# Two passes of 256 columns, in two banks, for the last 128 tokens of a decoder trunk's last product

## The chip, the cores and the metric

The kernel runs on one core of a Trainium2 chip. Its engines work side by side and wait for each other through semaphores: TensorE (PE in the profile) multiplies, with its weight loads shown apart as PEld; VectorE (DVE), ScalarE (ACT) and GpSimd (POOL) do elementwise work; SyncE (SP) issues transfers. The metric is the device time of one execution in microseconds (us); a kernel's time is the median of its runs.

## The reference

The input is 256 tokens of 2048 float32 features. Two layers follow each other, each with a token mixer (block attention in the first, retention in the second) and a gated feed-forward part. What ends the computation, and what the change touches, is this:

```python
def layer_norm(x, g, b):
    mu = xf.mean(-1, keepdims=True)
    var = jnp.square(xf - mu).mean(-1, keepdims=True)
    return ((xf - mu) * lax.rsqrt(var + LN_EPS)).astype(x.dtype) * g + b
...
    f = conv_ffn(h, ...)            # ... gelu(g) * val, w_out: (256 x 5632) @ (5632 x 2048)
    h = layer_norm(DEEPNORM_ALPHA * h + f, ln_g[i, 1], ln_b[i, 1])
```

## The kernel before

The 256 tokens are two tiles of 128 (TT = 2, tile index t); token t*128+p lives in partition p of `h[:, t]`. A matrix product is made in blocks of 512 output columns (COLS), and a block's rows of weights come in chunks of 256 rows by 512 columns. SP loads a chunk into one of four slots of `raw`; ACT rounds it to `w_hi` (L663), DVE subtracts to get the rest, `w_lo` (L943), and PE multiplies. Every product of the matrices is three matmuls: high by high, high by low and low by high (L328, L330, L331 in `multiply_tile`), each with 128 tokens of the activations as the stationary operand and 512 columns of weights as the moving one, accumulated in a bank of PSUM of 128 x 512 float32. `acc_a`, `acc_b`, `acc_c` and `mid` are pairs of such banks, one per token tile; `acc_a` and `acc_b` are the two halves of the tensor `acc_ab`, `acc_c` and `mid` those of `acc_cm`.

The last product of the program (`last_product`) is the fourth block of 512 columns of the second feed-forward part, 22 chunks into `acc_b`. The first 14 chunks are multiplied for both tiles as they arrive. The last eight are held on the chip: four in a place of their own (`early_hi`, `early_lo`, split ahead by L961) and four in the ring. PE passes over the eight chunks first for tile 0, then for tile 1. A pass is 8 chunks x 2 x 3 = 48 matmuls. Behind the first pass it signals `first_tile`, behind the second `products`.

DVE closes each tile in `last_layer_norm`: `last_residual` waits for the tile's signal, computes h = ALPHA*h + acc_b (L1079), takes the statistics of the last 512 columns (L1085), and joins the four blocks' statistics into mean and variance (L1088). GpSimd makes the reciprocal root from it (L917, L920). DVE meanwhile subtracts the mean and multiplies by the gain (`center`, L1094), and then scales and adds the bias (`scale_shift`, L1102), block by block; SP and ACT store each finished block (L285) in turn. `STORES` cuts tile 1's last block into two pieces of 256 columns. DVE and the other engines run their instructions strictly in the order written.

Of the kernel before, what the change touches and what calls it, by code (L numbers as in the profile page):

```python
# [24 lines left out]
ALU = mybir.AluOpType  # L25
# [3 lines left out]
P = 128  # L29
D = 2048  # L30
SEQ = 256
DEPTH = 2
TT = SEQ // P
KT = D // P
COLS = 512
CK = 2
CHUNK = CK * COLS
RING = 4
# [7 lines left out]
FSTEPS = F // COLS  # L46
NBLK = D // COLS
ALPHA = float((2 * DEPTH) ** 0.25)
# [17 lines left out]
TOKENS, FEATURES = (0, 0), (32, 48)  # L66
SLOT = CHUNK + 64
AHEAD = 4
FIRST_DONE = [None, 1, 2, 3, 4]
# [3 lines left out]
HCH = FT // CK  # L73
XQ, RQ = XCH // RING, RCH // RING
OQ = 2 * HCH // RING
# [11 lines left out]
Q_OUT1 = Q_FFN1 + 2 * FSTEPS * XQ - 1  # L87
TURNS = Q_OUT1 + NBLK // 2 * OQ


EARLY_FROM = [None, (Q_WO + 2 * XQ, XCH), (Q_OUT0 + OQ, HCH + 12), (Q_RWO + 3 * RQ, RCH - 2 * RING),
              (Q_OUT1 + OQ, HCH + 6)]
# [17 lines left out]
NC_FFN1 = NC_RET + RHEADS  # L110
# [4 lines left out]
B_USED = [None, NB_OUT0, NB_RET, NB_OUT1, NB_OUT1 + NBLK // 2]  # L115
# [4 lines left out]
def position(i, early):  # L120

    return i if early is None or i < early else i + min((i - early) // 2, RING)
# [8 lines left out]
def build_trunk(nc, x, weights, attn_tab, causal, ident_in, ret_tab, decay_tab, conv_in, ln_g, ln_b, out):  # L131
    with ExitStack() as ctx:
        def sb(name, shape, dt=F32):
            return ctx.enter_context(nc.sbuf_tensor(name, shape, dt))

        def sem(name):
            return ctx.enter_context(nc.semaphore(name))


        h = sb("h", [P, TT, D])  # L140
# [5 lines left out]
        w_lo = sb("w_lo", [P, RING, SLOT], F32R)  # L146
        conv_par = sb("conv_par", [P, DEPTH, 2 * FT, 4])
        ident = sb("ident", [P, P])
        ln_stats = sb("ln_stats", [P, TT, NBLK, 6])
        ln_mv = sb("ln_mv", [P, TT, 2])  # L150
        ln_ve = sb("ln_ve", [P, TT])
        ln_rstd = sb("ln_rstd", [P, TT])
# [42 lines left out]
        hid_hi, hid_lo = views(arena_at, ("hid_hi", [P, FT, SEQ], F32R), ("hid_lo", [P, FT, SEQ], F32R))  # L195
# [20 lines left out]
        acc_a, acc_b, acc_c, mid = acc_ab[:, 0:2], acc_ab[:, 2:4], acc_cm[:, 0:2], acc_cm[:, 2:4]  # L216

        def parts(s, place):

            return [w[:, s, at:at + CHUNK].rearrange("p (k n) -> p k n", k=CK)  # L220
                    for w, at in zip((w_hi, w_lo), place)]
# [27 lines left out]
        ln_params_in = sem("ln_params_in")  # L249
        out_stored = sem("out_stored")  # L250
        hi_ready = sem("hi_ready")
        lo_ready = sem("lo_ready")
        products = sem("products")
        first_tile = sem("first_tile")
        a_free, b_free, c_free = sem("a_free"), sem("b_free"), sem("c_free")
# [19 lines left out]
        tile0_turned, tile0_hi, tile0_ready = sem("tile0_turned"), sem("tile0_hi"), sem("tile0_ready")  # L275
        rv_rounded, s_rounded, s_ready = sem("rv_rounded"), sem("s_rounded"), sem("s_ready")
        half_set, idle_set = sem("half_set"), sem("idle_set")

        block = ctx.enter_context(nc.Block())

# [38 lines left out]

        @block.tensor  # L320
        def _(pe):
            def multiply_tile(acc, t, weight_parts, xh, xl, kt, first):

                o = acc[:, t]
                c = slice(t * P, (t + 1) * P)
                wh, wl = weight_parts
                for k in range(CK):
                    pe.matmul(o, xh[:, kt + k, c], wh[:, k], start=first and k == 0, stop=False,  # L328
                              skip_group_check=True)
                    pe.matmul(o, xh[:, kt + k, c], wl[:, k], start=False, stop=False, skip_group_check=True)  # L330
                    done = pe.matmul(o, xl[:, kt + k, c], wh[:, k], start=False, stop=True,  # L331
                                     skip_group_check=True)
                return done
# [25 lines left out]
            def product(turn, chunks, acc, free, used, xh, xl, feature_major, slots={}, ready=None, at=0,  # L359
                        early_at=None, held=None, first=0):  # L360


                if free is not None:
                    pe.wait_ge(free, used)
                hold = 0 if held is None else RING

                def count(s):
                    return RING * turn + position(at + s, early_at) + 1

                def counts(s):  # L370
                    return position(at + s + 1, early_at) - position(at + s, early_at)

                for s in range(chunks - hold):
                    if ready is not None:
                        pe.wait_ge(ready[0], ready[1](s))
                    multiply(acc, count(s), (at + s) % RING, xh, xl, CK * (first + s), feature_major,
                             first + s == 0, counts(s))
                    for step in slots.get(s, ()):
                        step()
                if hold:  # L380
                    for s in range(chunks - hold, chunks):
                        pe.wait_ge(lo_ready, count(s))
                        done = multiply_tile(acc, 0, parts((at + s) % RING, TOKENS), xh, xl, CK * s, False)
                    done.then_inc(first_tile, 1)
                    for s in range(chunks - hold, chunks):
                        multiply_tile(acc, 1, parts((at + s) % RING, TOKENS), xh, xl, CK * s,
                                      False).then_inc(products, counts(s))
                        for step in held.get(chunks - s, ()):
                            step()

            def last_product(turn, used):

                eh, el = early[4]
                split = HCH - 2 * RING

                def count(s):
                    return RING * turn + position(HCH + s, EARLY_FROM[4][1]) + 1

                product(turn, split, acc_b, b_free, used, hid_hi, hid_lo, False, at=HCH, early_at=EARLY_FROM[4][1])
                pe.wait_ge(lo_ready, early_position(4, RING - 1) + 1)  # L400
                for t in range(TT):
                    for s in range(RING):
                        done = multiply_tile(acc_b, t, (eh[:, s], el[:, s]), hid_hi, hid_lo, CK * (split + s), False)
                    for s in range(RING):
                        pe.wait_ge(lo_ready, count(split + s))
                        done = multiply_tile(acc_b, t, parts((HCH + split + s) % RING, TOKENS), hid_hi, hid_lo,
                                             CK * (split + RING + s), False)
                    done.then_inc((first_tile, products)[t], (1, RING)[t])

            def x_tiles(stage):  # L410
                return (x_ready, lambda s: PIECES * stage + s + 2)
# [527 lines left out]
        def _(dve):  # L939
# [45 lines left out]
            wh, wl = parts(0, FEATURES)  # L985
# [88 lines left out]
            def last_residual(stage, t, done, count, wait=True):  # L1074


                c = slice(D - COLS, D)
                dve.wait_ge(done, count)
                dve.scalar_tensor_tensor(out=h[:, t, c], in0=h[:, t, c], scalar=ALPHA, in1=acc_b[:, t],  # L1079
                                         op0=ALU.mult, op1=ALU.add).then_inc(b_free if t else summed, 1)  # L1080
                if t == 0:
                    dve.wait_ge(summed, NBLK * stage)
                else:
                    dve.wait_ge(b_free, B_USED[stage])
                dve.bn_stats(ln_stats[:, t, NBLK - 1], h[:, t, c]).then_inc(ln_stat, 1)  # L1085

                dve.wait_ge(ln_stat, TT * NBLK * stage - 1 + t)
                dve.bn_aggr(ln_mv[:, t], ln_stats[:, t].rearrange("p a s -> p (a s)")).then_inc(ln_mean, 1)  # L1088
                if wait:
                    dve.wait_ge(ln_mean, TT * (stage - 1) + t + 1)  # L1090

# [5 lines left out]
            def scale_shift(stage, part, t, c):  # L1097

                dve.wait_ge(ln_part, PART_BEFORE[stage] + part + 1)
                if c.start == 0:  # L1100
                    dve.wait_ge(ln_scale, TT * (stage - 1) + t + 1)
                dve.scalar_tensor_tensor(out=h[:, t, c], in0=h[:, t, c], scalar=ln_rstd[:, t:t + 1],  # L1102
                                         in1=ln_bias[:, c], op0=ALU.mult, op1=ALU.add).then_inc(ln_done, 1)
# [44 lines left out]

            def last_layer_norm(stage):

                dve.wait_ge(ln_params_in, 32 * NBLK * stage)
                for t, (done, count) in ((0, (first_tile, FIRST_DONE[stage])), (1, (products, RING * TURNS))):
                    mine = [i for i in range(len(STORES)) if STORES[i][0] == t]
                    last_residual(stage, t, done, count)
                    center(stage, mine[0], *STORES[mine[0]])
                    for i in mine:
                        if i + 1 in mine:
                            center(stage, i + 1, *STORES[i + 1])
                        scale_shift(stage, i, *STORES[i])

            def x_slots():

# [266 lines left out]
```

## Time and profile before

| What | Value |
|---|---|
| median of 3 runs | 2611.12 us (2610.8 to 2611.41) |
| the profiled execution's own time | 2612.95 us |
| its span, first to last instruction | 2611.2 us |
| mean granted TensorE clock | 0.999 |
| PE busy | 2598.4 us, 100% of the span |
| DVE, ACT, POOL busy | 1606.7, 1200.9, 15.9 us |

The span is shorter than the execution's own time by 1.75 us, which lie around it. Most of the program is one uninterrupted row of matmuls; what can be won or lost in the part looked at here are the PE passes up to the last matmul, and the work of DVE, GpSimd and the stores behind it.

### The profile page before, as it was taken

The numbers are of one execution on the slowest core, as the hardware profiler recorded it, in microseconds if no ns is written. First come the engines' busy times: TensorE is split into PE (matmuls) and PEld (weight loads), VectorE is DVE, ScalarE is ACT, GpSimd is POOL, SyncE is SP. The second block draws the span as 40 slices with busy tenths as digits, with TensorE's granted clock in tenths as the row PEclk, the third lists the DMA queues.
The fourth block names the chain that finished last, engine by engine and source line by source line (L and its number), as shares of the span: only waits on it lengthen the run. The fifth ranks groups of instructions, "written<-read, shape, count | busy, mean of one in ns | idle before, by whom it ended". The sixth has DMA issues, their size and how long they took to land.

```text
span 2611.2 us, 40543 instructions
## 1 busy us (share of the span) xinstructions
PE 2598.4 (100%) x14360; PEld 2265.8 (87%) x14360; DVE 1606.7 (62%) x1810; ACT 1200.9 (46%) x1348; POOL 15.9 (1%) x39
## 2 busy tenths in 40 slices
PE   9999999999999999999999999999999999999998
PEld 9999888888888888888888888888888888888886
DVE  6566667666676654565555555555766666665455
ACT  4444444555555543444444344433455555554332
POOL 0000000000000000000000000000000000000000
PEclk9999999999999999999999999999999999999999
DMA  6555574555555566655555555566555555556554
GB/s 226 180 166 166 172 252 146 194 186 191 193 186 191 189 230 193 206 186 181 179 174 181 181 177 179 181 216 198 170 193 181 194 183 193 192 193 229 195 188 153
DMA packets 140860, 493.92 MB, mean 189 GB/s; under 512 B 15472, under 2 KB 18032, under 8 KB 140784
## 3 DMA queue, kind: packets, MB, share of 16 engines
q1 hardware_dynamic: 133552, 481.49, 56.0%
q10 hardware_dynamic: 7232, 11.37, 1.4%
q8 instruction: 54, 0.88, 0.1%
q14 instruction: 22, 0.18, 0.0%
HBM read 490.70 MB, written 2.10 MB: 189 GB/s over the span
## 4 chain that ended last, share of the span: by engine, by line
PE 99%; DVE 0%; POOL 0%; ACT 0%; issue 0%; DVEq 0%; POOLq 0%
PE acc_cm L421 12%; PE acc_ab L331 12%; PE acc_ab L328 12%; PE acc_ab L330 12%; PE acc_ab L421 11%; PE acc_cm L424 6%; PE acc_ab L424 6%; PE acc_ab L342 5%; PE acc_ab L345 5%; PE acc_ab L344 5%; PE acc_cm L331 3%; PE acc_cm L328 3%; PE acc_cm L330 3%; PE acc_cm L484 0%; PE acc_cm L614 0%; PE acc_cm L635 0%
## 5 line engine op out<-in xcount | busy, mean ns | idle before, releaser
L943 DVE TENSOR_TENSOR w_lo<-raw,w_hi 128x1024 fp32r<-128x1024 f32 x895 | 1086.2, 1223 | 803.5 <-ACT w_hi L663 796.3
L663 ACT ACTIVATE w_hi<-raw 128x1024 fp32r<-128x1024 f32 (+1 forms) x897 | 934.9, 1055 | 877.6 <-PE acc_ab L331 447.1
L421 PE MATMUL acc_cm<-x_parts,w_hi 128*128 128x512 f32 x1408 | 489.4, 392 | 0.0
L421 PE MATMUL acc_ab<-x_parts,w_hi 128*128 128x512 f32 x1280 | 444.6, 392 | 0.0
L424 PE MATMUL acc_cm<-x_parts,w_lo 128*128 128x256 f32 x1408 | 394.3, 280 | 0.0
L424 PE MATMUL acc_ab<-x_parts,w_lo 128*128 128x256 f32 x1280 | 358.4, 280 | 0.0
L421 PEld LDWEIGHTS acc_cm<-x_parts,w_hi 128*128 128x128 f32 x1408 | 264.4, 188 | 57.8
L342 PE MATMUL acc_ab<-x_parts,w_hi 128*128 128x256 f32 x1024 | 291.1, 284 | 0.8 <-DVE w_lo L943 0.8
L345 PE MATMUL acc_ab<-x_parts,w_lo 128*128 128x256 f32 x1024 | 286.8, 280 | 0.0
L421 PEld LDWEIGHTS acc_ab<-x_parts,w_hi 128*128 128x128 f32 x1280 | 240.3, 188 | 52.6
L344 PE MATMUL acc_ab<-x_parts,w_hi 128*128 128x256 f32 x1024 | 285.8, 279 | 0.0
L328 PE MATMUL acc_ab<-w_hi,hid_hi 128*128 128x512 f32 x688 | 267.8, 389 | 0.0
L330 PE MATMUL acc_ab<-w_lo,hid_hi 128*128 128x512 f32 x688 | 267.7, 389 | 0.0
L331 PE MATMUL acc_ab<-w_hi,hid_lo 128*128 128x512 f32 x688 | 267.6, 389 | 0.0
L424 PEld LDWEIGHTS acc_cm<-x_parts,w_lo 128*128 128x128 f32 x1408 | 265.4, 189 | 0.1
L424 PEld LDWEIGHTS acc_ab<-x_parts,w_lo 128*128 128x128 f32 x1280 | 241.3, 188 | 0.0
L342 PEld LDWEIGHTS acc_ab<-x_parts,w_hi 128*128 128x128 f32 x1024 | 192.5, 188 | 1.5 <-issue 1.0
L344 PEld LDWEIGHTS acc_ab<-x_parts,w_hi 128*128 128x128 f32 x1024 | 192.7, 188 | 0.5
L345 PEld LDWEIGHTS acc_ab<-x_parts,w_lo 128*128 128x128 f32 x1024 | 192.5, 188 | 0.0
L330 PEld LDWEIGHTS acc_ab<-w_lo,hid_hi 128*128 128x128 f32 x688 | 129.1, 188 | 26.8
L331 PEld LDWEIGHTS acc_ab<-w_hi,hid_lo 128*128 128x128 f32 x688 | 129.1, 188 | 26.8
L328 PEld LDWEIGHTS acc_ab<-w_hi,hid_hi 128*128 128x128 f32 x688 | 129.1, 188 | 26.8
(142 smaller groups left out, 2976.6 us busy)
## 6 DMA issues: line engine op xcount, KB each, us to landing
raw<-in_weights_dram SPq DMA_DIRECT2D x911, 512.0 KB, 4.1
ln_gain<-in_ln_g_dram ACTq DMA_DIRECT2D x16, 256.0 KB, 4.6
ln_bias<-in_ln_b_dram ACTq DMA_DIRECT2D x16, 256.0 KB, 6.1
h<-in_x_dram SPq DMA_DIRECT2D x3, 512.0 KB, 8.9
decay_sb<-in_decay_tab_dram ACTq DMA_DIRECT2D x1, 1024.0 KB, 6.9
out_dram<-h SPq DMA_DIRECT2D x4, 256.0 KB, 2.5
out_dram<-h ACTq DMA_DIRECT2D x3, 256.0 KB, 2.5
raw<-in_weights_dram SPq DMA_DIRECT2D x2, 256.0 KB, 3.8
```

What stands on the lines that cost most here:

```text
L328: pe.matmul(o, xh[:, kt + k, c], wh[:, k], start=first and k == 0, stop=False, skip_group_check=True)
L330: pe.matmul(o, xh[:, kt + k, c], wl[:, k], start=False, stop=False, skip_group_check=True)
L331: done = pe.matmul(o, xl[:, kt + k, c], wh[:, k], start=False, stop=True, skip_group_check=True)
L342: pe.matmul(o, wh[:, k, c], xh[:, kt, :], start=first and f % 2 == 0, stop=False, skip_group_check=True)
L344: pe.matmul(o, wh[:, k, c], xl[:, kt, :], start=False, stop=False, skip_group_check=True)
L345: last = pe.matmul(o, wl[:, k, c], xh[:, kt, :], start=False, stop=True, skip_group_check=True)
L421: pe.matmul(acc[:, f], wh[:, k, c], x_parts[:, CK * s + k].rearrange("p a n -> p (a n)"), start=s == 0 and k == 0, stop=False, skip_group_ ...
L424: last = pe.matmul(acc[:, f, SEQ:2 * SEQ], wl[:, k, c], x_hi[:, CK * s + k, :], start=False, stop=True, skip_group_check=True)
L663: return act.activation(o, i, ACT.Copy)
L943: dve.tensor_tensor(wl, raw[:, at % RING], wh.bitcast(F32), ALU.subtract).then_inc(lo_ready, 1)
```

## The change

Tile 0's pass stays as it is. Tile 1's pass over the eight held chunks becomes two passes, each over the same eight chunks and over all their rows: the first multiplies the left 256 of the 512 columns into the first bank of `acc_c`, the second the right 256 into the second bank of `acc_c`, both starting from zero. The sum of tile 1 is thus in two places: the 14 chunks before in `acc_b[:, 1]`, the held eight in `acc_c`. DVE adds the first part, with ALPHA*h, as soon as the 14 chunks are done, in an instruction that now stands ahead of tile 0's closing work. It adds each half of 256 columns when its pass ends, takes each half's statistics by itself, and joins five sets of statistics in place of four for tile 1. `ln_stats` grows by one set a tile, which moves the tensors behind it by 64 bytes in each partition.

```diff
-        ln_stats = sb("ln_stats", [P, TT, NBLK, 6])
+        ln_stats = sb("ln_stats", [P, TT, NBLK + 1, 6])
...
+        first_half, half_summed = sem("first_half"), sem("half_summed")
...
-            def multiply_tile(acc, t, weight_parts, xh, xl, kt, first):
+            def multiply_tile(acc, t, weight_parts, xh, xl, kt, first, cols=slice(0, COLS), bank=None):
...
-                o = acc[:, t]
+                o = acc[:, t if bank is None else bank, 0:cols.stop - cols.start]
                 c = slice(t * P, (t + 1) * P)
-                wh, wl = weight_parts
+                wh, wl = [w[:, :, cols] for w in weight_parts]
...
+                def held_pass(acc, t, cols, bank, first):
+                    for s in range(RING):
+                        multiply_tile(acc, t, (eh[:, s], el[:, s]), hid_hi, hid_lo, CK * (split + s), first and s == 0,
+                                      cols, bank)
+                    for s in range(RING):
+                        pe.wait_ge(lo_ready, count(split + s))
+                        done = multiply_tile(acc, t, parts((HCH + split + s) % RING, TOKENS), hid_hi, hid_lo,
+                                             CK * (split + RING + s), False, cols, bank)
+                    return done
+
                 product(turn, split, acc_b, b_free, used, hid_hi, hid_lo, False, at=HCH, early_at=EARLY_FROM[4][1])
                 pe.wait_ge(lo_ready, early_position(4, RING - 1) + 1)
-                for t in range(TT):
-                    for s in range(RING):
-                        done = multiply_tile(acc_b, t, (eh[:, s], el[:, s]), hid_hi, hid_lo, CK * (split + s), False)
-                    for s in range(RING):
-                        pe.wait_ge(lo_ready, count(split + s))
-                        done = multiply_tile(acc_b, t, parts((HCH + split + s) % RING, TOKENS), hid_hi, hid_lo,
-                                             CK * (split + RING + s), False)
-                    done.then_inc((first_tile, products)[t], (1, RING)[t])
+                held_pass(acc_b, 0, slice(0, COLS), 0, False).then_inc(first_tile, 1)
+                pe.wait_ge(c_free, NC_FFN1 + FSTEPS)
+                held_pass(acc_c, 1, slice(0, COLS // 2), 0, True).then_inc(first_half, 1)
+                held_pass(acc_c, 1, slice(COLS // 2, COLS), 1, True).then_inc(products, RING)
...
+                def half_residual(n, done, count):
+
+                    c = slice(D - COLS + n * COLS // 2, D - COLS + (n + 1) * COLS // 2)
+                    dve.wait_ge(done, count)
+                    dve.tensor_tensor(h[:, 1, c], h[:, 1, c], acc_c[:, n, 0:COLS // 2], ALU.add).then_inc(half_summed, 1)
+                    dve.wait_ge(half_summed, n + 1)
+                    dve.bn_stats(ln_stats[:, 1, NBLK - 1 + n], h[:, 1, c]).then_inc(ln_stat, 1)
+
+                dve.wait_ge(products, RING * Q_OUT1 + RING * OQ + position(2 * HCH - 2 * RING, EARLY_FROM[4][1]))
+                dve.scalar_tensor_tensor(out=h[:, 1, last], in0=h[:, 1, last], scalar=ALPHA, in1=acc_b[:, 1],
+                                         op0=ALU.mult, op1=ALU.add).then_inc(b_free, 1)
+                dve.wait_ge(ln_params_in, 32 * NBLK * stage)
+                last_residual(stage, 0, first_tile, FIRST_DONE[stage])
+                normalise(0)
+                dve.wait_ge(b_free, B_USED[stage])
+                half_residual(0, first_half, 1)
+                half_residual(1, products, RING * TURNS)
+                dve.wait_ge(ln_stat, TT * NBLK * stage + 1)
+                dve.bn_aggr(ln_mv[:, 1], ln_stats[:, 1].rearrange("p a s -> p (a s)")).then_inc(ln_mean, 1)
+                dve.wait_ge(ln_mean, TT * stage)
+                normalise(1)
```

Here `normalise` is the old loop of `center` and `scale_shift` over a tile's stores. On PE, at the place where tile 0's pass ends and tile 1's begins, the program before reads as follows (the number at the end is partitions by columns written):

```order
L330 MATMUL acc_ab<-w_lo,hid_hi 128x512
L331 MATMUL acc_ab<-w_hi,hid_lo 128x512
L328 MATMUL acc_ab<-early_hi_90,hid_hi 128x512
L330 MATMUL acc_ab<-early_lo_91,hid_hi 128x512
L331 MATMUL acc_ab<-early_hi_90,hid_lo 128x512
```

And of the changed kernel, at the same place:

```order
L331 MATMUL acc_ab<-w_lo,hid_hi 128x512
L332 MATMUL acc_ab<-w_hi,hid_lo 128x512
L329 MATMUL acc_cm<-early_hi_90,hid_hi 128x256 [waits c_free]
L331 MATMUL acc_cm<-early_lo_91,hid_hi 128x256
L332 MATMUL acc_cm<-early_hi_90,hid_lo 128x256
```

Lines 328, 330 and 331 of before are 329, 331 and 332 of the changed kernel. From here on PE had 48 matmuls of 512 columns to its end and now has 96 of 256 columns; its first one waits for `c_free`, the release of `acc_c` by the feed-forward part's last sum.

On DVE, behind the last splits of chunks (L943), before:

```order
L943 TENSOR_TENSOR w_lo<-raw,w_hi 128x1024 [waits hi_ready,products] x4
L1079 SCALAR_TENSOR_TENSOR h<-h,acc_ab 128x512 [waits first_tile,ln_params_in]
L1085 BN_STATS ln_stats<-h 128x6 [waits summed]
```

and then, behind tile 0's last two scalings:

```order
L1102 SCALAR_TENSOR_TENSOR h<-h,ln_rstd,ln_bias 128x512 [waits ln_part] x2
L1079 SCALAR_TENSOR_TENSOR h<-h,acc_ab 128x512 [waits products]
L1085 BN_STATS ln_stats<-h 128x6 [waits b_free]
L1088 BN_AGGR ln_mv<-ln_stats 128x2 [waits ln_stat]
L1094 SCALAR_TENSOR_TENSOR h<-h,ln_mv,ln_gain 128x512 [waits ln_mean]
```

The changed kernel has at the first of these places:

```order
L950 TENSOR_TENSOR w_lo<-raw,w_hi 128x1024 [waits hi_ready,products] x4
L1177 SCALAR_TENSOR_TENSOR h<-h,acc_ab 128x512 [waits products]
L1086 SCALAR_TENSOR_TENSOR h<-h,acc_ab 128x512 [waits first_tile,ln_params_in]
```

and at the second:

```order
L1109 SCALAR_TENSOR_TENSOR h<-h,ln_rstd,ln_bias 128x512 [waits ln_part] x2
L1172 TENSOR_TENSOR h<-h,acc_cm 128x256 [waits first_half,b_free]
L1174 BN_STATS ln_stats<-h 128x6 [waits half_summed]
L1172 TENSOR_TENSOR h<-h,acc_cm 128x256 [waits products]
L1174 BN_STATS ln_stats<-h 128x6 [waits half_summed]
L1186 BN_AGGR ln_mv<-ln_stats 128x2 [waits ln_stat]
L1101 SCALAR_TENSOR_TENSOR h<-h,ln_mv,ln_gain 128x512 [waits ln_mean]
```

The sum over 512 columns has moved ahead of tile 0's work; in its place stand two pairs of a sum and statistics over 256 columns, of which one pair waits for the first of tile 1's two passes and only the other for the last matmul. The order on ACT, POOL and SP is unchanged.

## Rows read from the trace of the kernel before

**Rows 1.** The page: span and busy time of each engine.

```profile
span 2611.2 us, 40543 instructions
PE 2598.4 (100%) x14360; PEld 2265.8 (87%) x14360; DVE 1606.7 (62%) x1810; ACT 1200.9 (46%) x1348; POOL 15.9 (1%) x39
```

**Rows 2.** The chain that ended last, from 2600.5 us on: start, us, what.

```profile
2600.79 0.24 PE acc_ab L331
2601.03 0.02 issue
2601.06 0.70 DVE h L1079
2601.76 0.02 issue
2601.78 0.71 DVE ln_stats L1085
2602.48 0.02 issue
2602.51 0.27 DVE ln_mv L1088
2602.78 0.02 issue
2602.80 1.24 DVE h L1094 x2
...
2608.08 0.40 DVEq L132
```

**Rows 3.** Timeline of PE and PEld around tile 1's pass: start, us, what.

```profile
2589.75 0.39 PE L331 MATMUL acc_ab<-w_hi,hid_lo 128*128 128x512 f32 x1
...
2589.98 0.39 PE L328 MATMUL acc_ab<-early_hi,hid_hi 128*128 128x512 f32 x1
...
2590.20 0.39 PE L330 MATMUL acc_ab<-early_lo,hid_hi 128*128 128x512 f32 x1
2590.21 0.19 PEld L331 LDWEIGHTS acc_ab<-early_hi,hid_lo 128*128 128x128 f32 x1
...
2600.63 0.39 PE L331 MATMUL acc_ab<-w_hi,hid_lo 128*128 128x512 f32 x1
```

**Rows 4.** Timeline of PE, 104.00 to 112.88 us: the first and last of 75.

```profile
104.00 0.28 PE L345 MATMUL acc_ab<-x_parts,w_lo 128*128 128x256 f32 x1
...
112.88 0.28 PE L344 MATMUL acc_ab<-x_parts,w_hi 128*128 128x256 f32 x1
```

**Rows 5.** Groups of PEld by line and shape: count, busy us, mean ns, idle.

```profile
L344 PEld LDWEIGHTS acc_ab<-x_parts,w_hi 128*128 128x128 f32 x1024 | 192.7, 188 | 0.5
```

**Rows 6.** Groups of DVE by line and shape, the whole program.

```profile
L983 DVE TENSOR_TENSOR x_parts<-acc_cm,x_parts 128x256 fp32r<-128x256 f32 x1 | 0.4, 424 | 0.0
L1079 DVE SCALAR_TENSOR_TENSOR h<-h,acc_ab 128x512 f32<-128x512 f32 x8 | 5.5, 687 | 18.4 <-PE acc_ab L331 18.2
L1085 DVE BATCH_NORM_STATS2 ln_stats<-h 128x6 f32<-128x512 f32 x8 | 5.6, 695 | 0.3
L1088 DVE BATCH_NORM_AGGREGATE ln_mv<-ln_stats 128x2 f32<-128x24 f32 x8 | 2.1, 264 | 0.3
L1296 DVE BATCH_NORM_AGGREGATE gn_mv<-gn_stats 128x2 f32<-128x6 f32 x16 | 1.9, 161 | 0.0
```

**Rows 7.** Timeline of DVE from the last split to tile 0's last scalings.

```profile
2580.46 1.23 DVE L943 TENSOR_TENSOR w_lo<-raw,w_hi 128x1024 fp32r<-128x1024 f32 x1 [1.50 <-ACT w_hi L663]
2590.25 0.69 DVE L1079 SCALAR_TENSOR_TENSOR h<-h,acc_ab 128x512 f32<-128x512 f32 x1 [8.56 <-PE acc_ab L331]
...
2596.01 1.40 DVE L1102 SCALAR_TENSOR_TENSOR h<-h,ln_rstd,ln_bias 128x512 f32<-128x512 f32 x2
2601.06 0.69 DVE L1079 SCALAR_TENSOR_TENSOR h<-h,acc_ab 128x512 f32<-128x512 f32 x1 [3.65 <-PE acc_ab L331]
```

**Rows 8.** Busy us of the engines in tile 1's pass; PEclk is the granted clock.

```profile
core 0: us, PE busy (x) PEld busy (x) DVE busy (x) ACT busy (x) POOL busy (x), PEclk, DMA share, GB/s
...
2590.00:2601.00 11.00, 11.00 (x49) 8.80 (x47) 7.06 (x11) 0.00 (x0) 1.06 (x2) 1.00 0.27 97
```

More of the change, by code:

```diff
@@ L1087, in last_residual @@
                 dve.wait_ge(ln_stat, TT * NBLK * stage - 1 + t)
-                dve.bn_aggr(ln_mv[:, t], ln_stats[:, t].rearrange("p a s -> p (a s)")).then_inc(ln_mean, 1)
+                dve.bn_aggr(ln_mv[:, t], ln_stats[:, t, 0:NBLK].rearrange("p a s -> p (a s)")).then_inc(ln_mean, 1)
                 if wait:
@@ L1149, in last_layer_norm, with normalise @@
             def last_layer_norm(stage):
-                dve.wait_ge(ln_params_in, 32 * NBLK * stage)
-                for t, (done, count) in ((0, (first_tile, FIRST_DONE[stage])), (1, (products, RING * TURNS))):
+                def normalise(t):
                     mine = [i for i in range(len(STORES)) if STORES[i][0] == t]
-                    last_residual(stage, t, done, count)
                     center(stage, mine[0], *STORES[mine[0]])
@@ L1159, in last_layer_norm @@
                         scale_shift(stage, i, *STORES[i])
+                last = slice(D - COLS, D)
+                def half_residual(n, done, count):
[17 more added lines that the diff above has]
+                normalise(1)
             def x_slots():
```

## Prediction

> **What bounds the kernel now.** I read the page first: PE is busy for all but 12.8 of the span's 2611.2 us [rows 1], so nearly all of the program is paced by the matmuls. Then the chain of waits, at its end [rows 2]: after the last matmul it runs over DVE alone: the sum L1079, the statistics L1085, their joining L1088, two `center` steps, the scalings, and from 2608.08 us DVE's own end and the last stores. So two stretches set the end here. One is PE's row of matmuls for tile 1, which begins the instant tile 0's ends: the starts 2589.75 and 2589.98 lie one step apart [rows 3]. The other is what DVE does between the last matmul and the first `center`. Any matmul made slower in the first, and any DVE work taken out of the second, counts in full. The granted clock is 1.00 through the pass, its higher level, 2.4 GHz [rows 8].
>
> **PE's part: two passes for one.** Removed: 48 matmuls of 512 columns. They start at 2589.98 and 2600.63 for the first and last, 47 steps: 10.65 / 47 = 0.2266 us a step [rows 3]. Added: 96 matmuls of 256 columns. The same kind of operands at 256 columns, with a weight load each, runs in the first stage: 75 matmuls from 104.00 to 112.88 us, 74 steps: 0.1200 us a step, over the starts of three chunks with their waits [rows 4]. Half of 0.2266 would be 0.1133, so each costs 6.7 ns more than half of its predecessor: a step is some 13 ns plus 0.417 ns a column (0.2266 - 0.1200 = 0.1066 over 256 columns), and the 13 ns are now paid 96 times instead of 48. The pass from its first start to its modelled end took 47 x 0.2266 + 0.39 = 11.04 us and will take 95 x 0.1200 + 0.28 = 11.68 us. That is **+0.64 us**. The 48 further weight loads are in this sum already: a load is 0.188 us long [rows 5] and yet the steps are 0.120, so loads run beside matmuls in the rows I take the price from.
>
> The Trainium skill (TensorE: Matmul & The Clock Gate, Back-to-back issue gap) gives the isolated gap as N/2.4 + 2.5 ns, 109 ns at 256 columns and 216 at 512. By it the two passes would cost 96 x 0.1092 against 48 x 0.2158, +0.12 us. The trace does not agree at either width: 120.0 and 226.6 ns.
>
> The new wait for `c_free` was met when the feed-forward loop's last sum left `acc_c`, three blocks of product earlier, so it is met long before; behind it on PE stands everything, but it costs nothing. The waits for `lo_ready` in the second of the two passes ask for counts that tile 0's pass has already seen. I take both at nothing; if such a wait cost one visible step of DVE's kind of 0.03 us, nine of them would add 0.3 us, and this end goes into the range.
>
> **DVE's part ahead of the last matmul.** The added sum L1177 (512 columns, 0.69 us by L1079 [rows 6]) waits for the 14 chunks and stands behind the last split, which ends at 2581.69. It is done by 2582.4, and DVE idled until 2590.25 [rows 7]: hidden, with 7.9 us left. It stands ahead of tile 0's sum, which would be late only if those were gone. Tile 0's work is the same and ends at 2597.41 (2596.01 + 1.40 [rows 7]). The first pass of tile 1 ends at about 2589.98 + 47 x 0.12 + 0.28 = 2595.90, so the first half's sum and statistics start when DVE is free, at 2597.4, and take 0.42 + 0.03 + 0.43 = 0.88 us: over at 2598.3. The second half is ready at 2601.66. Cover of 3.4 us: hidden, and their price without it would be 0.9 us.
>
> **DVE's part behind the last matmul.** Removed: L1079 at 0.687 and L1085 at 0.695. Added: a `tensor_tensor` of 256 columns from PSUM, which L983 shows at 0.424 [rows 6]; statistics over 256 columns, which no row shows. The sum's two widths give 0.263 us for 256 columns (0.687 - 0.424), and the statistics' 512 cost 8 ns more than the sum's, so I take 0.695 - 0.265 = 0.43. Its bounds are 0.35, half of the wide one with no fixed part, and 0.695, no less than now. The joining gets 30 numbers a partition in place of 24. 6 numbers take 161 ns and 24 take 264 [rows 6], so 5.7 ns each and 34 ns more: 0.298 us. The gaps between the three, 0.02 to 0.03 us each [rows 2], stay. So the sum gives 0.263 and the statistics 0.265 back, the joining takes 0.034: **-0.49 us**; bounds -0.58 and -0.23.
>
> What follows (the root on GpSimd, which the second `center` covers, the scalings, the stores) is the same set of instructions, only moved as a whole. The 64 bytes by which the arena with `hid_hi` and `hid_lo` moves change no count and no width; I take them at nothing.
>
> **The sum.** +0.64 - 0.49 = +0.15 us on a span of 2611.2 us. The profiled execution took 2612.95, 1.83 above the median of the runs; the difference goes on the median: 2611.12 + 0.15 = **2611.3 us**. The two measurable pieces nearly cancel: halving the moving width pays the fixed part of a matmul 48 more times, and halving the tail of sum and statistics spares 512 columns of DVE work at about 1.03 ns each.
>
> **The rivals.**
> - *The matmul's fixed part is smaller here than in the first stage* (there the stationary operand is the weight, here the activation). At the least a matmul of 256 columns costs half of one of 512, 0.1133 us; then the passes take as long as before and DVE's gain stands alone: 2611.12 - 0.49 = 2610.6. Against it: at 512 columns this very stretch shows the same 13 ns over 512 x 0.417 [rows 3]. Chance 0.06. The gap that the Trainium skill gives, above, would come out here, at 2610.75.
> - *The change doesn't spare DVE what it says.* Statistics of 256 columns cost like 512, or the first half's pair is not done when the last matmul ends. The first gives +0.64 - 0.23 = +0.41, 2611.5; the second adds up to 0.9: 2612.2. For the second DVE would have to be 3.4 us later than rows 7 have it. Chance 0.08.
> - *The shift of tensors or of code touches the long part.* Every one of 2590 us stands on that: 0.02% of it is 0.5 us either way. Nothing in the profile speaks for it: PE's row is unbroken. Chance 0.04.
> - *Slower beyond doubt: the weight loads come out from under the matmuls.* A pass now asks for a load every 0.12 us, where tile 1's had one every 0.227, and a load is 0.188 us long [rows 5]. Were they not overlapped here, a matmul would take 0.188 for the load and 0.107 for 256 columns at 0.417 ns, 0.295 us, 96 of them 28.3 us against 10.9: +17.4 us, and 2628. It passes the 0.2% bound from a step of 0.175 us on (5.2 + 10.9 over 96 is 0.168, and DVE's 0.49 comes on top: 0.173). Against it: the 0.1200 of rows 4 with the same load each. Chance 0.01. The same page of the Trainium skill, on row and column tiling (The mechanism), lists that weight loads overlap matmuls in flight only where the row group differs; all loads here use all 128 rows, so by that this would be the outcome. The trace disagrees: loads of 0.19 us stand inside matmuls of full height at 2590.21 [rows 3].
>
> **How the numbers follow.** The forecast, +0.15 with a few tenths to each side, has 0.81. A measurement of this kernel can tell about 0.2%, 5.2 us, from no change; the whole of the two stretches touched is 11.0 us of PE and 1.7 us of DVE, so within 0.2% has 0.97, slower 0.02 (the loads, or a stall of the kind that I don't see), faster 0.01: to gain 5.2 us, more than all DVE work between the last matmul and the first `center` would have to go. The range takes in -0.49 of the first rival, +0.41 with the waits' 0.3 on it, +0.71, and the runs' own spread of 0.3 each way: 2610.3 to 2612.2.
>
> **What would show it.** Right: 96 matmuls on `acc_cm` with steps of 0.120, starting at about 2590.0 and ending at 2601.7; the first L1172 at about 2597.4 without idle time before it; the second about 0.04 behind the last matmul; L1174 at about 0.43, L1186 at 0.30; the first `center` of tile 1 at about 2602.95 instead of 2602.80. Wrong: steps off 0.120, a break between the passes, L1174 near 0.69, the first L1172 late, or matmul starts before 2590 that are not those of before.

## The result, and the profile after

The changed kernel takes 2634.14 us at the median of 6 runs (2633.08 to 2643.26), the kernel before 2611.26 (6 runs, 2610.66 to 2611.44): a ratio of 1.0098, 95% interval 1.0081 to 1.0115. It is slower by 23 us, where 0.15 was forecast. Ratios here and below are estimated from all runs of a kernel, so they are not quite the quotient of two medians. The profiled execution took 2633.08 us. The page of the changed kernel, its span and the busy time of each engine:

```profile
span 2631.3 us, 40643 instructions
PE 2619.0 (100%) x14408; PEld 2267.6 (86%) x14408; DVE 1607.5 (61%) x1813; ACT 1200.6 (46%) x1348; POOL 15.9 (1%) x39
```

The span is 20.1 us longer than in [rows 1], PE's busy time 20.6 us; the weight loads have 1.8 us more, and no other engine has a microsecond more. The granted clock is 0.999 in both. First the end of the program, which is all that the change edits; DVE's timeline from the last split on:

```profile
2600.78 1.23 DVE L950 TENSOR_TENSOR w_lo<-raw,w_hi 128x1024 fp32r<-128x1024 f32 x1 [1.57 <-ACT w_hi L670]
2601.92 0.68 DVE L1177 SCALAR_TENSOR_TENSOR h<-h,acc_ab 128x512 f32<-128x512 f32 x1
2610.89 0.69 DVE L1086 SCALAR_TENSOR_TENSOR h<-h,acc_ab 128x512 f32<-128x512 f32 x1 [8.29 <-PE acc_ab L332]
...
2616.64 1.40 DVE L1109 SCALAR_TENSOR_TENSOR h<-h,ln_rstd,ln_bias 128x512 f32<-128x512 f32 x2
2617.97 0.41 DVE L1172 TENSOR_TENSOR h<-h,acc_cm 128x256 f32<-128x256 f32 x1
...
2621.70 0.42 DVE L1172 TENSOR_TENSOR h<-h,acc_cm 128x256 f32<-128x256 f32 x1 [2.86 <-PE acc_cm L332]
2622.16 0.43 DVE L1174 BATCH_NORM_STATS2 ln_stats<-h 128x6 f32<-128x256 f32 x1
2622.62 0.29 DVE L1186 BATCH_NORM_AGGREGATE ln_mv<-ln_stats 128x2 f32<-128x30 f32 x1
2622.94 1.44 DVE L1101 SCALAR_TENSOR_TENSOR h<-h,ln_mv,ln_gain 128x512 f32<-128x512 f32 x2
```

and PE's, the first and the last of tile 1's 96 matmuls:

```profile
2610.61 0.28 PE L329 MATMUL acc_cm<-early_hi,hid_hi 128*128 128x256 f32 x1
...
2621.39 0.28 PE L332 MATMUL acc_cm<-w_hi,hid_lo 128*128 128x256 f32 x1
```

The added sum L1177 is hidden (8.29 us of idle time stand behind it), the first half's pair follows tile 0's last scaling at once, and the second half's sum starts 0.03 us behind the modelled end of the last matmul. From the first matmul of tile 1 to the first `center` of tile 1 it is 2622.94 - 2610.61 = 12.33 us; before it was 2602.80 - 2589.98 = 12.82 [rows 2, 3]. So the touched end is 0.49 us *shorter*, and the loss lies ahead of it: the first matmul of tile 1 starts at 2610.61 where it started at 2589.98, 20.63 us later, in a part of the program in which no instruction was changed.

To find where, I followed the chain of waits through both kernels by its landmarks, the transposes. In the kernel before:

```profile
425.11 0.87 PE acc_ab L585 x8
...
1187.72 1.31 PE acc_cm L614 x8
...
1679.69 1.31 PE acc_cm L614 x8
...
1897.61 0.87 PE acc_ab L585 x8
```

In the changed kernel:

```profile
426.90 0.87 PE acc_ab L592 x8
...
1196.38 1.31 PE acc_cm L621 x8
...
1688.65 1.31 PE acc_cm L621 x8
...
1911.56 0.87 PE acc_ab L592 x8
```

The lag is 1.79 us, then 8.66, 8.96, 13.95, and 20.63 at tile 1's pass. It grows in some stretches and hardly in others (0.3 us in the 492 us of the retention stage), and PE waits in none of them. The groups by line and shape name the matmuls. The kernel before:

```profile
L328 PE MATMUL acc_ab<-w_hi,hid_hi 128*128 128x512 f32 x688 | 267.8, 389 | 0.0
L328 PE MATMUL acc_ab<-w_hi,y_hi 128*128 128x512 f32 x256 | 99.8, 390 | 0.0
L331 PE MATMUL acc_cm<-w_hi,x_parts 128*128 128x512 f32 x384 | 149.8, 390 | 0.0
```

The changed kernel:

```profile
L431 PE MATMUL acc_cm<-x_parts,w_lo 128*128 128x256 f32 x1408 | 394.2, 280 | 0.0
L329 PE MATMUL acc_ab<-w_hi,hid_hi 128*128 128x512 f32 x680 | 269.0, 396 | 0.0
L329 PE MATMUL acc_ab<-w_hi,y_hi 128*128 128x512 f32 x256 | 101.4, 396 | 0.0
L332 PE MATMUL acc_cm<-w_hi,x_parts 128*128 128x512 f32 x384 | 149.7, 390 | 0.0
```

The matmuls whose stationary operand is `hid` or `y` went from 389 and 390 to 396 ns; those with `x_parts` stand where they were. These means hold the modelled end; the step from start to start is cleaner. PE's timeline of the changed kernel in the middle of the first down-projection, 13 steps apart:

```profile
999.95 0.39 PE L329 MATMUL acc_ab<-w_hi,hid_hi 128*128 128x512 f32 x1
...
1002.98 0.40 PE L331 MATMUL acc_ab<-w_lo,hid_hi 128*128 128x512 f32 x1
```

That is 3.03 / 13 = 0.2331 us a step where tile 1's pass showed 0.2266 [rows 3]; over longer rows the two values are 233.3 and 226.7 ns. `hid_hi`, `hid_lo`, `y_hi`, `y_lo` and the attention's output all lie in `arena`. The matmuls of 512 columns that have their stationary operand there are 2064 of `hid`, 768 of `y` and 384 of the attention: 3216, and 3216 x 6.67 ns = 21.4 us. By stretch: the attention's 384 make 2.6 (1.79 measured), 1056 of `hid` 7.0 (6.87), 768 of `y` 5.1 (4.99), the last 1008 of `hid` 6.7 (6.68). The 0.8 us by which the first misses is of the size of what a start drifts between executions: e1 below has tile 1's pass begin 0.43 us later than [rows 3] with every step as before.

### The profile page after: what moved, and what is told of

It reads as the page before. It is cut to its first block, busy times and chain, and to the rows that moved or that the text cites. A ratio compares the mean times of both kernels' runs of the same rounds, so it can differ in the third digit from the quotient of the medians.

```text
span 2631.3 us, 40643 instructions
## 1 busy us (share of the span) xinstructions
PE 2619.0 (100%) x14408; PEld 2267.6 (86%) x14408; DVE 1607.5 (61%) x1813; ACT 1200.6 (46%) x1348; POOL 15.9 (1%) x39
## 4 chain that ended last, share of the span: by engine, by line
PE 99%; DVE 0%; DMA 0%; SPq 0%; POOL 0%; issue 0%; ACT 0%; DVEq 0%; POOLq 0%
PE acc_cm L428 12%; PE acc_ab L332 12%; PE acc_ab L329 12%; PE acc_ab L331 12%; PE acc_ab L428 11%; PE acc_cm L431 6%; PE acc_ab L431 6%; PE acc_ab L343 5%; PE acc_ab L346 5%; PE acc_ab L345 5%; PE acc_cm L332 3%; PE acc_cm L329 3%; PE acc_cm L331 3%; PE acc_cm L491 0%; PE acc_cm L621 0%; PE acc_cm L642 0%
## 5 line engine op out<-in xcount | busy, mean ns | idle before, releaser
L431 PE MATMUL acc_cm<-x_parts,w_lo 128*128 128x256 f32 x1408 | 394.2, 280 | 0.0
```

Source lines behind the costliest of these rows:

```text
L431: last = pe.matmul(acc[:, f, SEQ:2 * SEQ], wl[:, k, c], x_hi[:, CK * s + k, :], start=False, stop=True, skip_group_check=True)
```

## The experiments

The only thing that the change alters for those matmuls is that `arena` lies 64 bytes further in each partition, as `ln_stats` grew from 192 to 240 bytes and the next tensor starts 64 bytes later. In the kernel before, `x_parts`, `w_hi` (as 512 columns are read from it) and `arena` all begin 128 bytes past a multiple of 256; in the changed one `arena` begins 192 past, and `side` behind it as well. The theory: the place of the arena against the weights makes each of these matmuls longer. The rival: something in the new tail or in the changed loops does. Tables give the median us of the runs, the ratio to the kernel before with its 95% interval, and the step of the 512-column matmuls on `hid`.

**The changed kernel, with arena and side put back, and the kernel before, with arena and side moved.**

```diff
# e1_arena_back, against the changed kernel
-        sb("align", [P, 32])
+        sb("align", [P, 16])
```

> The changed kernel, but with 64 bytes fewer in the pad ahead of the arena, so that arena and side lie again where they lay before (128 past a multiple of 256, as w_hi and w_lo do). Theory place (the 64 bytes by which the arena moved make each of some 3,200 matmuls whose stationary operand lies in the arena 6.7 ns slower, 21 us in all): about 2611 us, steps 0.2267 again, the tail's own effect -0.5 to +0.2. Rival code (the added instructions, the two banks or the two semaphores slow the long part): stays at 2633.

```diff
# e2_stats_only, against the kernel before
-        ln_stats = sb("ln_stats", [P, TT, NBLK, 6])
+        ln_stats = sb("ln_stats", [P, TT, NBLK + 1, 6])
...
-                dve.bn_aggr(ln_mv[:, t], ln_stats[:, t].rearrange("p a s -> p (a s)")).then_inc(ln_mean, 1)
+                dve.bn_aggr(ln_mv[:, t], ln_stats[:, t, 0:NBLK].rearrange("p a s -> p (a s)")).then_inc(ln_mean, 1)
```

> The kernel before with one thing of the change: ln_stats has a fifth set a tile, unused, which moves arena and side by 64 bytes. Theory place: 2631 to 2634 us, steps 0.2333 on hid, y and o. Rival code: 2611.

| Kernel | median, runs | ratio | step |
|---|---|---|---|
| e1_arena_back | 2611.50, 11 | 1.0001 (0.9992 to 1.0010) | 226.7 ns |
| e2_stats_only | 2643.89, 4 | 1.0135 (1.0119 to 1.0150) | 233.3 ns |

This settles the cause: with `arena` and `side` back, the whole of the change costs nothing that the medians can show; with the two moved and nothing else, the kernel before is slower. Which of the two tensors does what is told apart further down (e7, e8). e1_arena_back is also the clean test of the forecast's sum. Its PE timeline, first and last of the 96:

```profile
2590.41 0.28 PE L329 MATMUL acc_cm<-early_hi,hid_hi 128*128 128x256 f32 x1
...
2601.80 0.28 PE L332 MATMUL acc_cm<-w_hi,hid_lo 128*128 128x256 f32 x1
```

and its DVE timeline behind them:

```profile
2602.12 0.42 DVE L1172 TENSOR_TENSOR h<-h,acc_cm 128x256 f32<-128x256 f32 x1 [3.48 <-PE acc_cm L332]
...
2603.03 0.29 DVE L1186 BATCH_NORM_AGGREGATE ln_mv<-ln_stats 128x2 f32<-128x30 f32 x1
2603.36 1.44 DVE L1101 SCALAR_TENSOR_TENSOR h<-h,ln_mv,ln_gain 128x512 f32<-128x512 f32 x2
```

11.39 / 95 = 0.1199 us a step, and 12.95 us from the first matmul to the first `center`, against 12.82 before: +0.13 us, where +0.15 was forecast. This stretch can be trusted to some 0.01 us: in e4, e7, e9, e12, e13 and e14 below, whose tail is that of before and whose `hid` has the old step, it is 12.83 each time. In e2_stats_only, the kernel before with the placement of the changed one, it is 13.15, so at that placement the change makes the end 0.8 us shorter (12.33).

e2_stats_only was even slower than the changed kernel, and than its forecast, by some 10 us, which the arena's matmuls don't explain. The group of the wide product (`wide_multiply`, the up-projection of the feed-forward parts, pairs of a 512- and a 256-column matmul) shows it; e2_stats_only:

```profile
L424 PE MATMUL acc_cm<-x_parts,w_lo 128*128 128x256 f32 x1408 | 396.3, 281 | 0.0
L328 PE MATMUL acc_ab<-w_hi,hid_hi 128*128 128x512 f32 x688 | 271.7, 395 | 0.0
```

394.2 us of the first kind became 396.3. A second effect, then, in matmuls whose operands did not move at all. It is taken up below.

**Where is the line: how far, which way, against what?** Each of these is the kernel before with one thing changed: the pad `align` (of 32 words) of another size, or everything moved together.

```diff
# e3_arena_128 (64), e9_arena_256 (96), e5_arena_32 (40), e6_arena_less_64 (16), e11_arena_less_32 (24)
-        sb("align", [P, 32])
+        sb("align", [P, 64])
```

```diff
# e4_all_64: h, x_parts, the weights, the arena and side all 64 bytes further
+        sb("shift", [P, 16])
         h = sb("h", [P, TT, D])
```

> The kernel before with arena and side moved by 128 bytes, from 128 to 0 past a multiple of 256. If what counts is a boundary of 128 bytes: 2611 us. If the place modulo 256 counts, or the distance from w_hi: slower, 2620 to 2635.

> The kernel before with a pad of 64 bytes ahead of h, which moves h, x_parts, raw, w_hi, w_lo, arena and side together by 64 bytes; the arena stands at the very address that it has in the changed kernel. If the address by itself counts, all token-major matmuls get the longer step: 2632 us or more, up to 2645 with those on x_parts. If the distance between stationary and moving operand counts: 2611 us.

> The kernel before with arena and side moved by 32 bytes. If the penalty comes with lines of 64 bytes: some step over 0.2267, 2620 to 2650 us. If 32 bytes are within what it doesn't feel: 2611 us.

> The kernel before with arena and side moved by 64 bytes the other way (192 modulo 256). A rule that is the same both ways gives 2632 or 2643 us with 0.2333; if sign matters, anything from below 2611 (a shorter fixed part than now) to 2650.

> The kernel before with arena and side moved by 256 bytes. If the distance counts modulo 256 bytes or a divisor of it: 2611 us, 0.2267. If it counts in itself, or modulo more: slower.

> The kernel before with arena and side moved by 32 bytes the other way. If places past a multiple of 64 are all as bad as plus 32, hid, y and o at 0.2333; if the sign counts as it did with 64 bytes, about 0.229 and 2620. A step under 0.2267 would be a kernel faster than before.

| Kernel | arena against weights | median, runs | ratio | step |
|---|---|---|---|---|
| e9_arena_256 | +256 B | 2611.84, 8 | 0.9997 (0.9986 to 1.0008) | 226.7 ns |
| e4_all_64 | 0, arena as in the changed kernel | 2611.65, 10 | 1.0000 (0.9991 to 1.0009) | 226.7 ns |
| e3_arena_128 | +128 B | 2646.27, 4 | 1.0133 (1.0118 to 1.0149) | 232.4 ns |
| e5_arena_32 | +32 B | 2652.11, 2 | 1.0151 (1.0122 to 1.0180) | 233.3 ns |
| e11_arena_less_32 | -32 B | 2650.46, 1 | no interval from a single run | 233.3 ns |
| e6_arena_less_64 | -64 B | 2620.85, 6 | 1.0034 (1.0020 to 1.0048) | 228.9 ns |

The times of e3, e5 and e11 also hold 18 us of the second effect, which is why e3 and e5 lie above their forecasts; those of e4, e6 and e9 hold nothing of it, and the steps on `hid` are free of it.

In e4_all_64 the arena begins at the very byte at which it begins in the changed kernel, and the time is that of before: its absolute place does not make the steps longer, its place against the other operands does. A distance of 256 bytes is as good as none, and one of 128 is not, so the distance seems to count modulo 256; other multiples were not tried. The sign counts too: -64 costs a third of what +64 costs, though -32 costs as much as +32. The steps are means of patterns that repeat: 231 and 236 ns in turn on `hid` in the changed kernel, 231.7, 225.9 and 229.3 ns through the three matmuls of a group in e6_arena_less_64. They are not noise around one value. What unit of the chip lies behind the 256 bytes, the runs don't show.

The distance of a matmul's own two operands is not all of it. In the retention stage 72 matmuls have the stationary operand in `side` and the moving one in `arena`. e2_stats_only moves both by the same 64 bytes, and yet two of the three groups get longer. The kernel before, then e2_stats_only:

```profile
L624 PE MATMUL acc_cm<-rv_hi,s_hi 128*128 128x512 f32 x24 | 9.3, 389 | 0.0
L626 PE MATMUL acc_cm<-rv_hi,s_lo 128*128 128x512 f32 x24 | 9.3, 389 | 0.0
```

```profile
L624 PE MATMUL acc_cm<-rv_hi,s_hi 128*128 128x512 f32 x24 | 9.5, 394 | 0.0
L626 PE MATMUL acc_cm<-rv_hi,s_lo 128*128 128x512 f32 x24 | 9.5, 396 | 0.0
```

These matmuls come nine at a time between products of `x_parts`, which did not move. So what runs around a matmul seems to count as well, over a few matmuls. In the changed kernel the mean step of the 72 went from 226.6 to 231.0 ns, and 72 x 4.4 ns is the 0.3 us of the retention stage.

**The weights moved after the arena.** If only the distance counts, moving the weights' place by 64 bytes with the arena must mend `hid` and break the products that have `x_parts` stationary, which stays.

```diff
# e10_w_64, against the kernel before
-TOKENS, FEATURES = (0, 0), (32, 48)
+TOKENS, FEATURES = (16, 16), (32, 48)
...
-        sb("align", [P, 32])
+        sb("align", [P, 48])
```

> The kernel before with arena and side moved by 64 bytes, as in the changed kernel, and with the token-major chunks of w_hi and w_lo moved by 64 bytes too (16 columns further in each slot), while x_parts stays. Theory distance (what counts is how far the stationary operand lies from the moving one, modulo something over 64 bytes): hid, y and o, now at distance 0 again, fall back to steps of 0.2267; the token-major matmuls on x_parts, some 1,970, now at a distance of 64, rise to 0.2333, 13 us in all: 2624 us. Rival address (the arena's place alone counts): hid, y and o stay at 0.2333, x_parts at 0.2267: 2632 or 2643.

Measured: 2635.19 us (2 runs), ratio 1.0086 (1.0057 to 1.0116). Its groups:

```profile
L328 PE MATMUL acc_ab<-w_hi,hid_hi 128*128 128x512 f32 x688 | 267.8, 389 | 0.0
L328 PE MATMUL acc_cm<-w_hi,x_parts 128*128 128x512 f32 x384 | 153.2, 399 | 0.0
```

The line with `x_parts` was 151.9 us and 396 ns before:

```profile
L328 PE MATMUL acc_cm<-w_hi,x_parts 128*128 128x512 f32 x384 | 151.9, 396 | 0.0
```

`hid` is mended with the arena still displaced, and `x_parts` is worse with its place untouched. But its steps became 229 ns in the mean (226, 229 and 232 in turn) and not 233.3: here the stationary operand lies 64 bytes *below* the moving one modulo 256, as in e6_arena_less_64, and the price is that one's. The forecast of 2624 was missed on both counts: some 5 us came of `x_parts` and not 13, and 18 us of this kernel's loss are the second effect, again.

The last pass of the same trace shows the distance within one row. Its stationary operand is `hid` throughout. The first 24 matmuls have the early weights as moving operand, which lie in the place of `x_parts` and did not move; the last 24 have the ring's, which moved with the arena. PE's timeline of e10_w_64:

```profile
2612.09 0.39 PE L328 MATMUL acc_ab<-early_hi,hid_hi 128*128 128x512 f32 x1
...
2617.69 0.39 PE L328 MATMUL acc_ab<-w_hi,hid_hi 128*128 128x512 f32 x1
...
2619.07 0.39 PE L328 MATMUL acc_ab<-w_hi,hid_hi 128*128 128x512 f32 x1
...
2622.92 0.39 PE L331 MATMUL acc_ab<-w_hi,hid_lo 128*128 128x512 f32 x1
```

The first 24 steps are 5.60 / 24 = 0.2333 us, the last 17 are 3.85 / 17 = 0.2265; between them lie some six steps of 0.230.

**The second effect: the pairs of the wide product.** They have two levels in all kernels, 346.7 ns a pair (229.6 for the 512 columns and 117.1 for the 256) and 353.3 (233.3 and 120.0). A feed-forward part has one or the other for the whole of its 1344 pairs but the first eight, which always have the short one: about 1344 x 6.67 ns = 9.0 us a part. Of the profiled executions, before, after, e1, e4, e6, e9 and e12 have both parts short, e3, e5, e7, e10, e11, e13 and e14 both long, and e2 and e8 a short first and a long second. The first theory was that `side` matters, which was moved too in e2, e3 and e5 and which holds what the eight gate transposes read. It was moved alone (e7_side_64), and held at its place modulo 256 while the arena moved (e8_arena_only_64).

```diff
# e7_side_64 ([P, 16]); e8_arena_only_64 ([P, 48], and align [P, 48]), against the kernel before
         arena_at = nc.sbuf_base - word * 2 * FT * SEQ
+        sb("gap", [P, 16])
         side = sb("side", [P, 2 * D])
```

> The kernel before with a gap of 64 bytes between arena and side: only side (with gate_tok, which eight transposes read once in each feed-forward part) moves. In the profiles so far the matmul pairs of a whole feed-forward part take 346.7 or 353.3 ns, and the change comes right behind those eight transposes. Theory transposes: hid, y and o stay at 0.2267, no 21 us; some executions have 353.3 in one or both parts, 10 us each: 2611, 2621 or 2631. Rival arena (what the arena holds sets this state too): all executions at 2611.

> The kernel before with the arena moved by 64 bytes and side by 256, so that side stands at its old place modulo 256. Theory transposes: hid, y and o at 0.2333, pairs at 346.7 in every execution: 2632 us and little spread. Rival arena: 2632, 2642 and 2652 mixed, as with both moved.

| Kernel | median, runs | ratio | `hid` step | pairs, first and second part |
|---|---|---|---|---|
| e7_side_64 | 2630.59, 4 | 1.0068 (1.0051 to 1.0085) | 226.7 ns | 353.3, 353.3 |
| e8_arena_only_64 | 2644.01, 4 | 1.0131 (1.0114 to 1.0149) | 233.3 ns | 346.7, 353.3 |

e7_side_64 is slower by 18.1 us, two parts of 9.0, with `hid` as before: the effects are two. But e8_arena_only_64 has a long part with `side` where it was, so `side` alone is not the condition: the theory's 2632 us with short parts did not come, and of the rival's mixture 2643 and 2652 did. Three of its four runs, 2643.60, 2643.95 and 2644.06, lie together and the fourth, 2652.73, one part above. The changed kernel's own are four at 2633.1 to 2634.5 and two at 2642.8 and 2643.3. Only one execution of each has a profile, so that these gaps are parts at the other level is read from the times alone: the same program seems to fall into one level or the other from run to run. The kernel before never did so in its 61 runs, 2610.4 to 2613.5. The profiled execution of the changed kernel has both parts short, which is why its loss is the arena's alone.

When does the level change? PE's timeline of e7_side_64 around the gate transposes:

```profile
422.56 0.39 PE L422 MATMUL acc_cm<-x_parts,w_hi 128*128 128x512 f32 x1
...
424.64 0.39 PE L422 MATMUL acc_cm<-x_parts,w_hi 128*128 128x512 f32 x1
...
424.98 1.04 PE L586 MATMUL acc_ab<-ident,gate_tok 128*128 128x128 f32 x8
...
426.20 0.40 PE L422 MATMUL acc_cm<-x_parts,w_hi 128*128 128x512 f32 x1
...
428.32 0.40 PE L422 MATMUL acc_cm<-x_parts,w_hi 128*128 128x512 f32 x1
```

The six pairs ahead of the transposes take 2.08 us, 0.3467 each; six behind them take 2.12, 0.3533 each. In the kernel before it is 2.08 on both sides. In the 0.9 us of the transposes the level is set, and it is kept to the end of the part's pairs, 1344 x 0.35 = 470 us. So I added a transpose, a repetition of the last one, which changes no data: to e7_side_64 (e12), to the kernel before (e13), and two to the kernel before (e14).

```diff
                     for f in range(4):
                         for t in range(TT):
                             done = pe.transpose(by_feature(acc_b)[:, f, t * P:(t + 1) * P],
                                                 gate_tok[:, t, f * P:(f + 1) * P], ident[:])
+                    done = pe.transpose(by_feature(acc_b)[:, 3, P:2 * P], gate_tok[:, 1, 3 * P:4 * P], ident[:])
```

> As e7 (only side moved by 64 bytes), with the last of the eight gate transposes done twice. Theory stream (the state is a position in the stream of loads and matmuls, set at the transposes and kept while PE never pauses): pairs may go to 346.7, 2611 us, since the ninth moves that position. Rival place (the new distance of side alone makes it): 353.3 in both parts, 2630 us.

> The kernel before with the last of the eight gate transposes done twice. Theory stream: pairs may go to 353.3, 2621 or 2631 us. Rival place: 346.7, and 2611.4 us with the two added transposes of 0.1 us.

> The kernel before with the last gate transpose done three times, ten in all. If two states alternate with each transpose: pairs of 346.7 again, 2611.6 us. If a third position exists: another value than 346.7 and 353.3; under 346.7 it would be a kernel faster than before.

| Kernel | transposes | median, runs | ratio | pairs |
|---|---|---|---|---|
| e12_side_ninth | 9, `side` moved | 2613.06, 8 | 1.0004 (0.9993 to 1.0015) | 346.7, 346.7 |
| e13_before_ninth | 9 | 2630.40, 3 | 1.0073 (1.0050 to 1.0096) | 353.3, 353.3 |
| e14_before_tenth | 10 | 2630.76, 3 | 1.0071 (1.0048 to 1.0094) | 353.3, 353.3 |

One more transpose takes the 18 us from the kernel with `side` moved and puts them on the kernel before. PE's timeline of e13_before_ninth, six pairs apart:

```profile
425.44 0.27 PE L587 MATMUL acc_ab<-ident,gate_tok 128*128 128x128 f32 x1
...
425.91 0.40 PE L421 MATMUL acc_cm<-x_parts,w_hi 128*128 128x512 f32 x1
...
428.03 0.40 PE L421 MATMUL acc_cm<-x_parts,w_hi 128*128 128x512 f32 x1
```

A transpose costs about 0.11 us itself (eight take 0.87 in the chain above); its effect is 9 us a part. That the pairs keep the level that they have behind the short burst is shown, and that one transpose more changes it, both ways. What the state is, and which addresses or counts lead to which level, is not: a tenth transpose does not bring the short level back, so it is not a matter of odd and even.

## Why the prediction was wrong, point by point

- **The step that failed**: "The 64 bytes by which the arena with `hid_hi` and `hid_lo` moves change no count and no width; I take them at nothing." The count and the width are indeed the same; the step from one matmul to the next is not. Measured: 6.67 ns on each of 3216 matmuls, 21.4 us, and in some runs 9 us more for a feed-forward part. e1 and e2 show it from both sides.
- **The rival that was right in kind**, "the shift of tensors or of code touches the long part", had 0.04, and a size of 0.5 us from a percentage picked without a row. Its reason, "Nothing in the profile speaks for it: PE's row is unbroken", was the wrong test: an unbroken row hides nothing, and so any change of its step counts in full. The 1% came in without one gap.
- **PE's term**, +0.64 us from 0.1200 and 0.2266 us a step: right with the arena in place (0.1199 in e1). There was luck in it: the first stage, from which the price was taken, has two levels too. From 159.54 to 162.10 us of the kernel before the same matmuls make 22 steps of 0.1164 us, and by them the term would have been +0.30. In the changed kernel the step is (2621.39 - 2610.61) / 95 = 0.1135 us, the value of the first rival, and the term vanishes. So in this pass the displaced arena goes with longer 512-column matmuls and shorter 256-column ones, in one trace of each kernel. The rival's reason was a smaller fixed part of the matmul; the prediction's one fixed part of 13 ns for both widths does not hold, as the wide product's 229.6 and 117.1 ns show too. Why the two widths go opposite ways stays open.
- **DVE's term**, -0.49 us: right. The sum of 256 columns took 0.42 (forecast 0.424), the statistics 0.43 (0.43), the joining of 30 numbers 0.29 (0.298).
- **The covers** held: L1177 and the first half's pair are hidden, the waits for `c_free` and `lo_ready` cost nothing, the pass is unbroken.
- **The sum**, +0.15: +0.13 in e1, whose ratio to the kernel before is 1.0001 (0.9992 to 1.0010). The interval cannot tell it from zero; the trace can (12.95 us against 12.83 in seven traces).
- **The weight loads** did not come out from under the matmuls: steps of 0.1199 and 0.1135 us stand beside loads of 0.192 and 0.188. (The 0.2% bound of that rival is passed from a step of 0.173 us on, as its own bracket has it, and not 0.175.) That 2628 lies near the result is chance: the 23 us have nothing to do with the stretch it was about.

## What to carry to other kernels

Where PE is busy for all of the span, look at the addresses of its operands after any edit that allocates, also one far from the hot loop, and compare the step of one long group of matmuls before and after; a lag that grows where nothing was edited is the sign. Here the cheapest row of 512-column matmuls had stationary and moving operand at the same place modulo 256 bytes (for tile 1's 256-column matmuls that place was the dearer one), and shrinking a pad by 64 bytes gave some 22 us back. Placement alone moved the time by up to 1.5% (e5), so treat a smaller saving as unproven until the edit has been timed with the placement held still.

## What the runs showed of the hardware

- The step of a 512-column matmul with a load of 128 columns depended on the distance of its stationary from its moving operand in a partition: 226.7 ns at 0 and +256 bytes, 233.3 at +32, +64 and -32, 232.4 at +128, 228.9 at -64. The Trainium skill (TensorE: Matmul & The Clock Gate, Step-by-step: what each phase is for) says that weights and moving operand are read through two independent ports, so that a load takes no read bandwidth from the running matmul. From that one would expect the distance not to matter; e4_all_64 against e2_stats_only shows that it does, with 6.67 ns, 3% of a step.
- The distance is not the whole rule: the 72 retention matmuls went from 226.6 to 231.0 ns with their own distance unchanged, and in e10's last pass the step needed some six matmuls to come down from 233.3 to 226.7 ns.
- Long rows of equal matmuls kept a few values, each the mean of a pattern that repeats: 113.5 and 119.9 ns at 256 columns for tile 1's pass, 346.7 and 353.3 for a pair of both widths. So the 0.1200 of [rows 4] is the value of one level, and the same matmuls of tile 1's pass fell on it in e1 and on another in the changed kernel.
- The pairs of the wide product kept their level for 470 us without a pause, and it was set in a burst of eight to ten transposes of 128 columns. Run times that lie 9 us apart for the same program fit one such part at the other level, so a kernel that hardly waits can still have runs in two groups.
